# The second FFN's first-layer slots: one 512-column product against two 256-column products per weight block

## The reference

```
def swiglu(u, w_in, w_out):
    gate, up = jnp.split(u @ w_in, 2, axis=-1)
    return (jax.nn.silu(gate) * up) @ w_out
...
u = modulate(rms_norm(h, norm_ffn[layer]), sh2, sc2)
h = h + g2[:, None, :] * swiglu(u, ffn_w_in[layer], ffn_w_out[layer])
```

## Time and profile before

| | |
|---|---|
| median of three executions | 2135.83 us |
| lowest, highest | 2133.03, 2143.2 us |
| span of the profiled execution (first to last instruction) | 2142.1 us |
| instructions | 26418 |
| TensorE matmul busy | 2069.3 us (97%) |
| TensorE weight load busy | 1758.7 us (82%) |
| DVE, ACT, POOL busy | 1286.0, 892.2, 263.3 us |
| mean granted TensorE clock | 0.988 of full |

### The profile page before, as it was taken

The page is one execution under the profiler, slowest core; times in us unless marked ns, Lnnn a source line. Parts: engine busy times, 40 slices in busy tenths (PEclk is TensorE's granted clock), DMA queues, the critical chain, the costliest instruction groups (busy, mean ns, idle before and its releaser), DMA issues.

```text
span 2142.1 us, 26418 instructions
## 1 busy us (share of the span) xinstructions
PE 2069.3 (97%) x10328; PEld 1758.7 (82%) x10328; DVE 1286.0 (60%) x1900; ACT 892.2 (42%) x1259; POOL 263.3 (12%) x280
## 2 busy tenths in 40 slices
PE   7999999999999999999999999998999998999997
PEld 3888888888888888866788888886688887888886
DVE  7877766454544562586545444588547766565656
ACT  5533343475656645466422222255134343322222
POOL 3000000054444413010000000001400000000000
PEclk9999999999999999999999999999999999999998
DMA  6642231445555533321132233222013222222321
GB/s 222 222 171 99 99 119 47 151 158 205 189 196 201 200 129 118 118 72 48 59 118 99 99 103 114 99 82 81 32 65 108 93 95 79 99 99 99 101 97 39
DMA packets 39484, 247.50 MB, mean 116 GB/s; under 512 B 4927, under 2 KB 5183, under 8 KB 11588
## 3 DMA queue, kind: packets, MB, share of 16 engines
q1 hardware_dynamic: 27940, 191.75, 25.8%
q0 software_dynamic: 8080, 47.79, 6.5%
q10 hardware_dynamic: 3344, 6.29, 0.8%
HBM read 239.52 MB, written 6.29 MB: 115 GB/s over the span
## 4 chain that ended last, share of the span: by engine, by line
PE 83%; DVE 8%; issue 3%; ACT 2%; POOL 2%; DVEq 0%; ACTq 0%; POOLq 0%
PE bank L762 24%; PE bank L763 23%; PE bank L764 23%; PE bank L1105 2%; DVE w_lo L2123 2%; ACT w_hi L1592 1%; PE bank L962 1%; PE bank L1233 1%; PE bank L1243 1%; PE bank L1254 1%; PE bank L801 1%; PE bank L942 1%; DVE scr L2196 1%; POOL pool L717 0%; ACT pool L1580 0%
## 5 line engine op out<-in xcount | busy, mean ns | idle before, releaser
L762 PE MATMUL bank<-u_hi,w_hi 128*128 128x512 f32 x1656 | 649.8, 392 | 13.9 <-DVE w_lo L2123 6.1
L763 PE MATMUL bank<-u_lo,w_hi 128*128 128x512 f32 x1656 | 630.7, 381 | 0.0
L764 PE MATMUL bank<-u_hi,w_lo 128*128 128x512 f32 x1656 | 630.5, 381 | 0.0
L2123 DVE TENSOR_TENSOR w_lo<-raw,w_hi 128x2048 fp32r<-128x2048 f32 x160 | 368.0, 2300 | 191.0 <-ACT w_hi L1592 190.7
L1592 ACT ACTIVATE w_hi<-raw 128x2048 fp32r<-128x2048 f32 x160 | 304.5, 1903 | 271.2 <-PE bank L764 258.0
L762 PEld LDWEIGHTS bank<-u_hi,w_hi 128*128 128x128 f32 x1656 | 315.1, 190 | 72.2 <-issue 17.4
L764 PEld LDWEIGHTS bank<-u_hi,w_lo 128*128 128x128 f32 x1656 | 314.8, 190 | 45.1
L763 PEld LDWEIGHTS bank<-u_lo,w_hi 128*128 128x128 f32 x1656 | 315.1, 190 | 44.7 <-issue 3.3
L762 PE MATMUL bank<-g_hi,w_hi 128*128 128x512 f32 x768 | 294.7, 384 | 6.4 <-DVE w_lo L2123 4.5
L763 PE MATMUL bank<-g_lo,w_hi 128*128 128x512 f32 x768 | 291.8, 380 | 0.0
L764 PE MATMUL bank<-g_hi,w_lo 128*128 128x512 f32 x768 | 291.6, 380 | 0.0
(11 more groups left out here) (311 smaller groups left out, 2307.9 us busy)
## 6 DMA issues: line engine op xcount, KB each, us to landing
raw<-in_wts SPq DMA_DIRECT2D x180, 1024.0 KB, 4.9
pool<-in_wts POOLq DMA_DIRECT2D x36, 1024.0 KB, 5.2
spectra<-pool ACTq DMA_DIRECT2D x16, 256.0 KB, 2.1
scr<-in_rel POOLq DMA_DIRECT2D x16, 256.0 KB, 3.1
pool<-spectra POOLq DMA_DIRECT2D x16, 256.0 KB, 3.1
H<-in_x ACTq DMA_DIRECT2D x1, 2048.0 KB, 14.8
out<-H SPq DMA_DIRECT2D x8, 256.0 KB, 2.0
pool<-in_window POOLq DMA_DIRECT2D x1, 1024.0 KB, 9.1
```

The lines of the kernel that those rows point to most:

```text
L762: pe.matmul(out, lh, rh, start=start, stop=False, skip_group_check=True)
L763: pe.matmul(out, lh, rl, start=False, stop=False, skip_group_check=True)
L764: return pe.matmul(out, ll, rh, start=False, stop=stop, skip_group_check=True)
L2123: dve.tensor_tensor(w_lo[RING[w]][:, :], raw[W_STREAM[w] % raw_ring][:, :], w_hi[RING[w]][:, :].bitcast(F32), ALU.subtract).then_inc(lo_do ...
```

## The change: what it does

Slots 1 to 21 of the second layer's `fi1` go through a new function in place of `slot_std`. It does one bank after the other, and each bank in two passes, one for each half of the 512 columns: first all 8 row blocks for columns 0 to 255, then all 8 for columns 256 to 511. A product has a moving operand of 256 columns. Each 128x128 weight block is therefore loaded twice. The first layer's FFN, slot 0 and the second-layer slots `fo1` stay as they are. The wait for the activations is one wait for all eight blocks, and each bank is claimed just ahead of its own first product.

```diff
+            def three_half(out, lh, ll, rh, rl, half, start, stop):
+
+                rh, rl = (halves_in_turn(x)[:, half * P:(half + 1) * P, :] for x in (rh, rl))
+                pe.matmul(out, lh, rh, start=start, stop=False, skip_group_check=True)
+                pe.matmul(out, lh, rl, start=False, stop=False, skip_group_check=True)
+                return pe.matmul(out, ll, rh, start=False, stop=stop, skip_group_check=True)
+
+            def slot_by_bank(label, i, first, count):
+
+                w, hi, lo = weights(label, i)
+                wait_u(count + KC)
+                for j in range(2):
+                    b = claim(first + j)
+                    for half in range(2):
+                        for k in range(KC):
+                            c = k * 256 + j * P
+                            mm = three_half(b[:, half * 256:(half + 1) * 256], hi[:, c:c + P], lo[:, c:c + P],
+                                            u_hi[:, k, :], u_lo[:, k, :], half, k == 0, k == KC - 1)
+                    complete(mm, first + j, w if j else None)
+                mods(w)
+
             def ffn(layer, ucount, gcount):
                 for g in range(FFN_G + 1):
                     if g < FFN_G:
                         for i in (2 * g, 2 * g + 1):
                             if i:
-                                slot_std(f"fi{layer}", i, FIRST[f"fi{layer}_{i}"], ucount)
+                                (slot_by_bank if layer == "1" else slot_std)(f"fi{layer}", i, FIRST[f"fi{layer}_{i}"], ucount)
                             else:
                                 slot_behind_norm(f"fi{layer}", FIRST[f"fi{layer}_0"], ucount)
```

## The result

The changed kernel takes 2147.18 us (median of 18 executions, 2140.41 to 2151.39) against 2135.77 us before (18 executions, 2132.57 to 2143.68). The ratio is 1.0044, with an interval of 1.0033 to 1.0054: 9.4 us more, between 7.0 and 11.5. The ratio is not the quotient of the two medians: these lie 11.4 us apart, and why the two differ is taken up under "Each kernel once more". The forecast was 2143.6 us, plus 7.8 us, counted as no change; the measured ratio lies inside the 0.5%, near its edge.

What follows compares the result with a forecast made beforehand. The prediction took TensorE's product cadence in the second FFN as the bound; plus 7.8 us for short products and nothing for the other parts took 2135.8 to 2143.6 us, range 2136 to 2160 us.

Steps and rivals of the forecast that it cites:

- What bounds the kernel: Second FFN stretch: TensorE alone is the bound, busy 345.7 of 349 us at full clock, so product cadence counts.
- Part 1: The 21 changed slots: twice the products and loads, one every 111.7 ns, set by the load; plus 7.8 us.
- Part 2: Gate bank in each changed slot: done half a slot earlier, moving the Silu but not the multiply; costed at nothing.
- Parts 3 and 4: Next slot's weights (4.3 us to spare), bank claims and waits in the second FFN: no cost.
- Rival A: Changed slots: the stream is the bound at 109.0 ns a product, plus 2.4 us, 2138 us; chance 0.17.
- Rival B: Changed slots: the load no longer hides, 190 or 216 ns a product, plus 166 or 218 us; chance 0.07.
- Rival C: Changed slots: long runs cost more than bursts, 114 to 124 ns a product, plus 12 to 33 us; chance 0.14.
- The carry to the whole: Whole kernel: plus 7.8 us carried from the profiled span to the median, 2135.8 to 2143.6 us, 0.37% more.
- A sign that was off: Second FFN stretch: the share of time filled by weight loads should rise above 95%.

Runs made afterwards that it cites:

- narrow_384_128: Changed kernel with passes of 384 and 128 columns, and only the first 64 block columns in products that don't open an accumulation; ratio 1.0040, median 2146.95 us.
- halves_together: Kernel before, in its old order, with each product cut into two consecutive 256-column products loading the same block twice; ratio 1.0050, median 2146.75 us.
- narrow_block: Changed kernel, but products that don't open an accumulation use only the first 64 columns of their weight block; ratio 1.0027, median 2141.25 us.
- uneven_384_128: Changed kernel with the two passes over a bank at 384 and 128 columns, full weight blocks; ratio 1.0305, median 2198.85 us.

## Why the prediction was right, point by point

- **What bounds the kernel.** Right: TensorE's cadence at full clock. The clock is 1.00 in the stretch in both profiles, and in each run the time added per product, times the number of products, showed in the stretch.
- **Part 1, the cadence.** The term was 111.7 ns from bursts of fp32 products. The new slots run at 111.7 ns without a pause for 10.72 us. The sum of 7.8 us became 7.55 in the stretch; the old slot measured between distant Silus is 10.36 us and not the 10.35 taken, which is 21 x 0.01 = 0.2 us of it. The choice of the row with the same load and the same stream time, over the stream's 109.0 ns, was what decided, and the runs with half a load and with uneven passes show that the reason was the right one. One step towards it doesn't carry: the 275 ns record of 128 fp32 columns was read as the length of their stream, but the uneven passes show that a 128-column load makes it 275 whatever streams under it. What does carry is the other pair, 380 ns for 256 fp32 columns and 379 for 512 fp32r columns, and the bursts' load spacing, which is 111.7 ns even beside one column. That the new records have 275 ns is right for another reason than the one given.
- **Part 2, the early gate bank.** Right: the Silu moved 5.4 us ahead of the multiply, and the order alone gave 341.02 us.
- **Parts 3 and 4.** Right: TensorE waits for weights in the same two places, 1.3 us at slot 1 and 2.4 us behind the FFN; `g_lo` ahead of fo 10 stays at 0.8 us.
- **Rival A** (stream-bound, 109.0 ns) is what the kernel with half loads does: 109.3 ns. The 0.11 us between two loads was too coarse to bear on it, as the prediction says. The 262 cycles of "TensorE: Matmul & The Clock Gate" in the Trainium skill (section "Back-to-back issue gap"; 109.2 ns) describe that kernel and not the change.
- **Rival B** (the load no longer hides) is refuted: at 190 or 216 ns the stretch would have grown by over 160 us. The sentence of the Trainium skill that loads overlap running products only where row groups differ ("TensorE: Matmul & The Clock Gate"; it stands in the section "The mechanism", not in the one that the prediction names) is contradicted by 111.7 ns with full-height blocks.
- **Rival C** (a long run costs more than a burst) is refuted for the stretch by 111.7 ns in both FFNs.
- **The carry to the whole.** 2143.6 us was forecast and 2147.18 measured, with a ratio that says plus 9.4 where the term says 7.6 to 7.8. That difference is inside the interval and inside the range. It comes with a lower mean granted clock outside the stretch, which the prediction carried over unchanged; what lowers it is open. That the result counts as no change has some luck in it: the ratio is 9.4 us, but the medians lie 11.4 us apart, past the 10.7 us of 0.5%, for which the prediction gave one chance in six.
- **A sign that was off:** weight loads were to fill over 95% of the stretch. They fill 335.85 of 357 us, 94%, since the fo slots in it keep their 512 columns.

## What to carry to other kernels

Before cutting a product's moving side, compare two times per product: the streaming of its columns and the load of its stationary block. With a fresh 128-column block each time, fp32r at 256 columns streams in 109.3 ns, just under the load's 111.7, and the slot takes 3.5% more than with 512 columns; a product of 128 columns still takes the load's 111.7 ns, where its stream needs 58 or less. To price a shape that a trace doesn't hold, look for another instruction in it with the same load and the same stream time, even of another type, and read start to start and not the length of the records: 275 ns records came every 111.7 ns.

## What the runs showed of the hardware

- A load costs by its columns: 111.7 ns start to start for 128 (the changed kernel), 58 for 64 (narrow_384_128), so (111.7 - 58) / 64 = 0.84 ns a column and some 4 ns fixed. Loading the block that was loaded last costs the same again (halves_together, 348.58 us in both orders).
- A stream costs its columns and a little: 109.3 ns for 256 (narrow_block), 162.3 for 384 (uneven_384_128), 215.7 for 512, each some 2.5 ns over columns / 2.4. With full blocks a product costs the larger of stream and load.
- The modelled record of a product grows when the load holds it: 128 fp32r columns have 222 ns beside 64-column loads and 275 beside 128-column loads, with the same stream; beside a 128-column load that ran under a wide product it is 0.22 us again. Equal records of 128 and 256 columns (275 and 275) are therefore no sign of an equal stream.
